# One inference step of a hybrid decoder: the order of TensorE's attention work inside the steps of the input projection

## The reference, cut to what matters

```python
n = rms_norm(x, g_mix); z = n @ w_in          # 320 x 2048 by 2048 x 4608
# A: gMLP gate, 4 groups of 128 channels, causal 128x128 mixing
# B: 16 heads x 64, three dilated windows; the sample tokens also see
#    a cache of 2048 keys and values, of which 1280 positions are reached
# M: 4 heads x 128 over 256 memory tokens (cached for the samples)
h = x + concat(ya, yb, ym) @ w_out
y = h + hier_moe(rms_norm(h, g_ffn))           # top 2 of 8 experts in top 1 of 4 groups
```

## Time and profile before

| | |
|---|---|
| runs | 1129.72, 1131.15, 1131.67 us; median 1131.15 |
| the profiled execution | span 1133.0 us from its first to its last instruction |
| PE (TensorE matmul) busy | 1048.4 us, 93% |
| PEld (weight loads) busy | 585.1 us, 52% |
| DVE (VectorE) busy | 546.4 us, 48% |
| ACT (ScalarE) busy | 203.2 us, 18% |
| chain that ended last | PE 71%, DMA 17%, DVE 8% |

### The profile page before, as it was taken

How to read it: one execution, slowest core, us unless ns; L and a number is a source line. 1 busy time by engine, 2 the same in 40 slices (tenths; PEclk the granted TensorE clock), 3 DMA queues, 4 the chain that set the end, 5 groups by cost and what they waited for, 6 DMA issues and landing times.

```text
span 1133.0 us, 17343 instructions
## 1 busy us (share of the span) xinstructions
PE 1048.4 (93%) x7193; PEld 585.1 (52%) x7193; DVE 546.4 (48%) x1075; ACT 203.2 (18%) x463; POOL 41.7 (4%) x39
## 2 busy tenths in 40 slices
PE   8999999999999999999999998999998869788887
PEld 3687776666666666677777542323332323222232
DVE  3775554665545556484624126435443434333432
ACT  1022103221212331312001111111111111111112
POOL 0030110001100000000000000000000000000000
PEclk9999999999999999999999999999999999999999
DMA  9899539989999999733857448999999999999996
GB/s 314 346 281 307 211 135 383 360 338 347 347 417 378 382 358 355 306 131 126 337 204 273 172 188 374 426 413 425 430 426 426 428 427 429 429 428 427 426 427 237
DMA packets 38981, 384.54 MB, mean 339 GB/s; under 512 B 4911, under 2 KB 7599, under 8 KB 10895
## 3 DMA queue, kind: packets, MB, share of 16 engines
q1 hardware_dynamic: 36336, 375.83, 82.7%
q0 software_dynamic: 1568, 5.62, 1.9%
q10 hardware_dynamic: 1008, 2.10, 0.6%
HBM read 375.63 MB, written 7.90 MB: 339 GB/s over the span
## 4 chain that ended last, share of the span: by engine, by line
PE 71%; DMA 17%; DVE 8%; ACT 2%; issue 2%; POOL 1%; SPq 0%; ACTq 0%; DVEq 0%; POOLq 0%
PE ps L619 24%; DMA arena<-w_gu 13%; PE ps L611 7%; PE ps L1088 6%; PE ps L1015 5%; PE ps L1126 4%; PE ps L1107 4%; DMA arena<-w_proj 4%; PE ps L812 4%; PE ps L601 3%; PE ps L779 3%; DVE cst L1894 1%; DVE cst L1827 1%; PE ps L1131 1%; PE ps L795 1%
## 5 line engine op out<-in xcount | busy, mean ns | idle before, releaser
L619 PE MATMUL ps<-arena 128*128 128x256 f32 x1456 | 332.9, 383 | 2.1 <-DVE arena L1431 1.7
L619 PEld LDWEIGHTS ps<-arena 128*128 128x128 f32 x1456 | 270.6, 190 | 52.0 <-issue 14.7
L1088 PE MATMUL ps<-arena,cst 128*32 128x512 f32 x1024 | 120.8, 606 | 30.2 <-DMA arena<-w_gu 28.5
L1894 DVE STREAM_TRANSPOSE cst<-ps 128x512 f32<-128x512 f32 x31 | 22.2, 717 | 173.5 <-PE ps L1015 173.5
L611 PE MATMUL ps<-arena 128*64 128x256 f32 x832 | 101.3, 386 | 0.0
L1015 PE MATMUL ps<-arena,cst 128*32 128x512 f32 (+1 forms) x768 | 93.3, 599 | 0.5 <-DVE cst L1823 0.5
L1088 PEld LDWEIGHTS ps<-arena,cst 128*32 128x32 f32 x1024 | 31.9, 111 | 114.6 <-issue 79.8
L1107 PE MATMUL ps<-arena,stat 128*32 128x512 f32 x512 | 64.8, 625 | 23.3 <-DVE stat L1898 23.2
L611 PEld LDWEIGHTS ps<-arena 128*64 128x64 f32 x832 | 55.1, 136 | 37.8 <-issue 14.2
L1924 DVE COPY arena<-ps 32x512 f32<-32x512 f32 x62 | 42.9, 691 | 41.9 <-PE ps L1107 40.6
L1404 DVE TENSOR_TENSOR arena<-arena 128x512 f32<-128x512 f32 x52 | 35.7, 687 | 53.1 <-PE ps L619 41.8
(11 more groups left out here) (284 smaller groups left out, 979.4 us busy)
## 6 DMA issues: line engine op xcount, KB each, us to landing
arena<-w_gu SPq DMA_DIRECT2D x64, 2048.0 KB, 29.3
arena<-w_dn SPq DMA_DIRECT2D x32, 2048.0 KB, 27.7
arena<-w_proj SPq DMA_DIRECT2D x43, 1024.0 KB, 7.9
arena<-kc SPq DMA_DIRECT2D x16, 2048.0 KB, 10.7
arena<-vc SPq DMA_DIRECT2D x16, 2048.0 KB, 9.0
arena<-w_o SPq DMA_DIRECT2D x16, 1024.0 KB, 4.9
arena<-kc SPq DMA_DIRECT2D x8, 1024.0 KB, 8.3
arena<-vc SPq DMA_DIRECT2D x8, 1024.0 KB, 9.4
```

The lines of the kernel that those rows point to most:

```text
L619: last = mm(psum[:, regions(v)[j - 1]], left[a], right[:, a], start=first and opens and a == 0, stop=final and a == 1, skip_group_check=True)
L1088: last = mm(ps[g:g + 32, 0, :], xgT[:, s % 2, kt, :], w[:, k, :], start=kt < 4, stop=kt >= KT - 4)
```

## The change

TensorE's 108 steps issue the same instructions with the same waits. What attention does in a step is sorted into three functions by shape. In steps with `s % 3 < 2`, whose product (L619) uses the whole array, the order is product, whole tiles, row halves, column groups. In steps with `s % 3 == 2`, whose product (L611) uses column groups of 64, it is product, column groups, row halves, whole tiles. No other engine's stream is edited.

```diff
+            def column_groups(s):
+                n, i = sample_step(s)
+                for p, at in enumerate(PAIR_AT):
+                    if s == at + 3:
+                        pair_values(p)
+                if n is not None and i <= 2:
+                    qk(n, i)
+                if n is not None and i >= 4:
+                    pv(n, i - 4)
+                if s == MEM_AT:
+                    memory_scores(0)
+                if s == MEM_AT + 2:
+                    memory_values(0)
+                    memory_scores(1)
+                if s == MEM_AT + 4:
+                    memory_values(1)
+            def row_halves(s):
+                for p, at in enumerate(PAIR_AT):
+                    if s == at:
+                        pair_scores(p)
+            def whole_tiles(s):
+                n, i = sample_step(s)
+                if n is not None and 3 <= i <= 5:
+                    turn_s(n, i - 3)
+                for u in range(NUNIT):
+                    if s == START[u] + 7:
+                        fold(u)
+                if s in (MEM_AT + 3, MEM_AT + 5):
+                    memory_fold((s - MEM_AT - 3) // 2)
+                if s in (MEM_AT + 1, MEM_AT + 3):
+                    memory_turn((s - MEM_AT - 1) // 2)
+                # mhead_scores, gate_products, mhead_values, mhead_turn, pair_turn, turn: as before, in this order
...
+                if t < 2:
+                    whole_tiles(s)
+                    row_halves(s)
+                    column_groups(s)
+                else:
+                    column_groups(s)
+                    row_halves(s)
+                    whole_tiles(s)
```

More of the change, by code:

```diff
@@ L900, in _ @@
                         mhead_scores(g)
[L901 to L924, removed]
                 if GATE_AT <= s < GATE_AT + G:
@@ L938, in _ @@
                         turn(k)
+            for s in range(UNITS_X):
+                ch, q, t = s // 12, s // 3 % QTR, s % 3
+                if ch == 0 and t == 0:
+                    pe.wait_ge(x_mixed, q + 1)
+                    if q == 0:
+                        pe.wait_ge(z_ready, 2)
+                if t == 0:
+                    plain_products(2 * QTR + s // 3, 1 + ch, xT, q, x_mix, q == 0, q == QTR - 1)
+                elif t == 1:
+                    mixed_products(2 * QTR + s // 3, 1 + ch, xT, q, x_mix, q == 0, q == QTR - 1)
+                else:
+                    small_unit(2 * QTR + s // 3, 7, HALF, xT, q, q == 0, q == QTR - 1)
+                if t < 2:
+                    whole_tiles(s)
+                    row_halves(s)
+                    column_groups(s)
+                else:
+                    column_groups(s)
+                    row_halves(s)
+                    whole_tiles(s)
             def turn_n2(ch, t):
```

## The result

The changed kernel's median is 1141.58 us (9 runs, 1136.11 to 1146.28), that of the kernel before 1131.58 (9 runs, 1129.72 to 1139.19). The ratio, estimated over all the runs, is 1.0072, 95% interval 1.0054 to 1.009: slower by 8.1 us (6.1 to 10.2). It is not the quotient of the two medians, which lie 10.0 us apart. The forecast was slower by 4.95, 1136.1 us, range 1132.2 to 1139.5: the direction is right, the size is not, and the time is outside the range.

What follows compares the result with a forecast made beforehand. TensorE's own stream was taken to bound the input projection; edge savings of -1.65, +0.30 for plain-step edges, exposed waits and -0.3 at step 51 sum to +4.95 us, giving 1136.1 us, range 1132.2 to 1139.5.

Steps and rivals of the forecast that it cites:

- the edges: Shape changes on TensorE cost about 0.10 us per side: -1.65 us over eleven mixed steps, +0.30 over six plain ones.
- the exposed waits: TensorE waits uncovered by reordering: step 66 +1.85, 94 +2.0, 96 +1.2, 97 +0.75, 99 +0.3, 49 +0.5 us.
- the delay of step 94: Scores start 2.45 us later, so ScalarE's chain and L1551 end later and step 96 waits: +1.2 us.
- (a): Edges alone: moved groups' inputs come early enough, -1.7 us, 1129.4 us; chance 0.06.
- (b): Absorbed later: the expert stage's weight waits take up the delay, time stays at 1131.2 us; chance 0.06.
- (c): Only direct exposures in steps 66, 94, 49, without chains in 96 to 100: +2.7 us, 1133.8; chance 0.12.
- above, the idle times of 2.6, 1.95 and 2.1 us might cost clock: Upper end of the range: new idle times in steps 66, 94 and 96 might lower TensorE's clock; not in the sum.
- (d): TensorE's clock falls after idle time: twice 1.7 us on top of the forecast, 1139.5 us; chance 0.10.

Runs made afterwards that it cites:

- eleven-step kernel: New order only in steps 37, 43, 46, 51, 55, 67, 70, 73, 85, 87, 91, against the kernel before: ratio 0.9981, -2.2 us.
- with the clock kept up: Whole change plus products that nobody reads in the idle times of steps 66, 94 and 96, against the kernel before: ratio 1.005, +5.7 us, trace +5.12.
- the run with step 94 alone: New order in step 94 only, its idle time filled with four unread products, against the kernel before: ratio 1.0041, +4.6 us, trace +2.49.
- step 66 alone: New order in step 66 only, against the kernel before: ratio 1.003, +3.4 us, trace +4.94; with five unread products 1.0015, trace +1.86.
- second run: The changed kernel again, unedited, against the kernel before: ratio 1.0068, +7.7 us, trace +8.08.

## Why the prediction was right and where it was wrong

**Right: the edges.** 0.15 us in seven of the mixed steps and 0.20 in three (43, 49, 73), with step 94's inside its 1.86; some 0.05 the other way in five of the plain ones, and 0.26 at step 84, where a wait of 0.22 comes in. The eleven-step kernel, -1.84 in the trace and -2.2 us (0.5 to 3.9 faster) in the timed runs, shows that they count at the end of the kernel.

**Right: the exposed waits.** Steps 66, 94, 96, 98, 100 and 50 came within 0.1 us each, and their sum with the edges is +5.12 with the clock kept up, forecast +4.95. The idle times themselves came out somewhat shorter than forecast in two places: 2.41 for 2.6 at step 66, and at step 98 the 0.82 and 0.20 for 1.2. That the delay of step 94 goes through ScalarE to step 96 is shown by the run with step 94 alone. Rivals (a), (b) and (c) are out: the inputs came when the trace said, nothing later took the delay back (611.84 and 611.81 us from step 107 on), and the chains count (step 96, 98 and 100).

**Wrong: the step "above, the idle times of 2.6, 1.95 and 2.1 us might cost clock".** It was priced as rival (d), with a chance of 0.10, two falls and 1.7 us each, and left out of the predicted time. The price of a fall was right (1.6 to 1.7, but 3.1 in the kernel with step 66 alone), the number and the chance were not: the clock fell behind all three in one profile, behind two in the other. 5.12 + 3 by 1.65 = 10.1 is the 9.98 of the first trace; 5.12 + 2 by 1.65 = 8.4 is near the 8.08 of the second. So the term for the clock, put at nothing in the sum, was 4.86 us of 9.98 in the first trace. The mechanism of (d) is what happened beside the forecast's own.

How I came to 0.10: "In the input projection the clock is 1.00 throughout" says nothing on idle times of 2 us there. In the stretch of the earlier trace rows the longest was 0.98. The stage begins earlier, at 63 us, and its longest idle time is this one, behind which the clock stayed at 1.00:

```profile
98.04 1.32 PE L619 MATMUL ps<-arena 128*128 128x256 f32 x5 [1.72 <-DVE arena L1431]
```

And from the expert stage I took one fall as a price and did not count how often one came: in the trace of the kernel before, two of seven idle times of 2.77 to 2.98 us had one.

## What to carry to other kernels

Before work is moved to the front of a step, look for each waiting instruction when its input is ready, not how long it waited before: at step 94 the wait read zero, because the work in front of it ended 0.05 us after the input. A rule on order, such as one shape beside its like, pays step by step, and the steps in which it exposes a wait are best left out. On TensorE an idle time of some 2 us in a stage that is otherwise dense has to be priced with the clock behind it, which here nearly doubled it. If it can't be avoided, products that nobody reads were cheaper than waiting (step 66 alone: 1.86 us for 4.94).

## What the runs showed of the hardware

In the input projection the clock fell behind six of seven idle times of 1.79 to 2.41 us (1.79, 2.00, 2.41 in the changed kernel; 1.79, 2.40, but not 1.82 in its second run; 2.40 with step 66 alone). It fell behind none of seven of 1.36 to 1.72 (1.36, 1.49, 1.54 above; 1.48, 1.52, 1.69 and 1.72 at the end of step 11 in four of the kernels).

These lengths hold for this stage only. In the expert stage of the kernel before:

```profile
755.03 3.49 PE L1107 MATMUL ps<-arena,stat 128*32 128x512 f32 x16 [0.69 <-DVE stat L1898]
978.74 1.92 PE L1088 MATMUL ps<-arena,cst 128*32 128x512 f32 x16 [2.98 <-DMA arena<-w_gu]
993.42 2.95 PE L1088 MATMUL ps<-arena,cst 128*32 128x512 f32 x16 [2.88 <-DMA arena<-w_gu]
```

Sixteen such matmuls take 1.92 us at full clock. So it stayed up behind 2.98 us, fell behind 2.88 (0.57 from 994 to 998), and fell behind 0.69 (0.57 from 755 to 759), where eight short matmuls of 32 columns (L1097) stood before the idle time. The same happened at 816.75 behind 0.76 (0.59 from 816 to 820). So the length of the idle time alone does not decide, and what else does was not tried.

After a fall TensorE's work ran at the lower level (1.2 GHz) in every shape that stood there: `qk(4, 0)` took 3.52 us for 1.85, and with step 66 alone the six transposes 1.90 for 1.21.

This agrees with the Trainium skill (TensorE: Matmul & The Clock Gate, What's actually happening), in that how busy the engine has been lately sets the throttle: here six of seven idle times of 1.79 us and more in a dense stage brought it on.

An edge between two tile shapes in float32 costs about 0.09 us on the handing over (the mixed product goes over after 3.46 without an edge and 3.55 with one) and about 0.10 inside the following group (3.65 with both), less where that group is short (0.06 for four transposes).

Steps 11 and 19 differed by up to 1.9 and 1.5 us between the profiled executions, with the same instructions. For step 11 the traces show why: ScalarE (L1163, in the changed kernel L1177) waits for a transfer of `x_rows` and only then evicts a chunk (L1178), VectorE's L1431 waits for that, and the product of step 12 for VectorE. In the kernel before L1163 starts 0.69 us behind the start of step 11, in the changed kernel 0.84 ahead of it. Step 19 was not followed up.
